# A depthwise convolution moved from two engines onto one, and eighteen PSUM copies moved to ScalarE

## The reference

```python
u, g, q, k, v, f = jnp.split(h, cuts, axis=-1)
a = u * jax.nn.sigmoid(g)
...
a_ext = jnp.concatenate([jnp.zeros((b, CONV_A_WIDTH - 1, CONV_A_CH), a.dtype), a], axis=1)
conv_out = conformer_tail(a_ext, w_dw_a[i], b_dw_a[i], ln_a_g[i], ln_a_b[i])
att = fox_prompt(q, k, v, lf)
```

## Time and profile before

| what | value |
|---|---|
| median of 3 runs | 2841.85 us (2841.03 to 2844.7) |
| the profiled execution, its own time | 2843.69 us |
| its span in the profile | 2842.0 us |
| busy: PE / DVE / ACT / POOL | 2632.0 / 1417.6 / 738.9 / 480.7 us |
| granted TensorE clock, mean | 0.953 |

### The profile page before, as it was taken

The page is one execution under the profiler, slowest core; times in us unless marked ns, Lnnn a source line. Parts: engine busy times, 40 slices in busy tenths (PEclk is TensorE's granted clock), DMA queues, the critical chain, the costliest instruction groups (busy, mean ns, idle before and its releaser), DMA issues.

```text
span 2842.0 us, 37619 instructions
## 1 busy us (share of the span) xinstructions
PE 2632.0 (93%) x15741; PEld 2537.0 (89%) x15741; DVE 1417.6 (50%) x1956; ACT 738.9 (26%) x1203; POOL 480.7 (17%) x436
## 2 busy tenths in 40 slices
PE   6987849897999999999999899989999999999995
PEld 5977737675999999999999789989999999999994
DVE  2699955555674333333333664457533333333356
ACT  3110135546342111111111431234311111111133
POOL 2189952221220000000000320023000000000022
PEclk8998968798999999999999999999999999999998
DMA  7111040016421111111111331133111111111131
GB/s 208 47 33 30 16 146 1 15 30 169 133 60 45 45 45 45 45 45 45 45 45 46 103 116 45 45 112 89 43 39 39 44 45 45 45 45 45 45 89 63
DMA packets 217916, 173.28 MB, mean 61 GB/s; under 512 B 9121, under 2 KB 195601, under 8 KB 217752
## 3 DMA queue, kind: packets, MB, share of 16 engines
q1 hardware_dynamic: 211488, 159.41, 19.1%
q0 software_dynamic: 4960, 11.49, 1.3%
q10 hardware_dynamic: 1320, 0.24, 0.1%
HBM read 152.45 MB, written 18.93 MB: 60 GB/s over the span
## 4 chain that ended last, share of the span: by engine, by line
PE 83%; DVE 9%; ACT 2%; issue 2%; DMA 1%; POOL 1%; SPq 1%; DVEq 0%; ACTq 0%; POOLq 0%
PE PS L664 24%; PE PS L665 24%; PE PS L666 24%; DVE CACC L1514 5%; PE PS L833 3%; PE PS L820 1%; PE PS L801 1%; DVE WLO L1430 1%; PE PS L805 1%; DMA RAW<-in_w_in_even 1%; DVE RSD L1709 1%; PE PS L678 1%; PE PS L679 1%; PE PS L672 0%; DVE Y L1717 0%
## 5 line engine op out<-in xcount | busy, mean ns | idle before, releaser
L664 PE MATMUL PS<-AH,WHI 128*128 128x368 f32 x3360 | 1126.3, 335 | 63.9 <-DVE QKV L1544 32.6
L665 PE MATMUL PS<-AL,WHI 128*128 128x368 f32 x3360 | 1119.9, 333 | 0.0
L666 PE MATMUL PS<-AH,WLO 128*128 128x368 f32 x3360 | 1115.5, 332 | 0.0
L664 PEld LDWEIGHTS PS<-AH,WHI 128*128 128x128 f32 x3360 | 639.8, 190 | 72.6 <-DVE QKV L1544 36.3
L665 PEld LDWEIGHTS PS<-AL,WHI 128*128 128x128 f32 x3360 | 638.5, 190 | 2.6 <-issue 0.6
L666 PEld LDWEIGHTS PS<-AH,WLO 128*128 128x128 f32 x3360 | 638.8, 190 | 0.0
L1774 DVE TENSOR_TENSOR HF<-S,PS 128x368 f32<-128x368 f32 x132 | 71.0, 538 | 678.5 <-ACT S L1067 678.5
L664 PE MATMUL PS<-HH,WHI 128*128 128x368 f32 x1056 | 353.4, 335 | 24.6 <-issue 16.7
L1052 ACT CAST WHI<-RAW 128x1024 fp32r<-128x1024 f32 x224 | 223.6, 1047 | 537.1 <-PE PS L666 530.7
L665 PE MATMUL PS<-HL,WHI 128*128 128x368 f32 x1056 | 352.8, 334 | 0.0
L666 PE MATMUL PS<-HH,WLO 128*128 128x368 f32 x1056 | 352.3, 334 | 0.0
(11 more groups left out here) (264 smaller groups left out, 2050.5 us busy)
## 6 DMA issues: line engine op xcount, KB each, us to landing
RAW<-in_w_ffn_gate SPq DMA_DIRECT2D x52, 512.0 KB, 3.9
RAW<-in_w_ffn_up SPq DMA_DIRECT2D x52, 512.0 KB, 4.9
RAW<-in_w_ffn_down SPq DMA_DIRECT2D x52, 512.0 KB, 3.6
RAW<-in_w_in_even SPq DMA_DIRECT2D x20, 512.0 KB, 5.0
Y<-x_spill SPq DMA_DIRECT2D x12, 736.0 KB, 8.2
RAW<-in_w_out_even SPq DMA_DIRECT2D x16, 512.0 KB, 4.6
RAW<-in_w_in_odd SPq DMA_DIRECT2D x16, 512.0 KB, 4.0
RAW<-in_w_out_odd SPq DMA_DIRECT2D x16, 512.0 KB, 4.8
```

The costliest lines, as they stand in the source:

```text
L664: pe.matmul(out, wh, xh, start=first, stop=False)
L665: pe.matmul(out, wh, xl, start=False, stop=False)
L666: return pe.matmul(out, wl, xh, start=False, stop=last)
```

## The change

VectorE convolves all four tiles, GpSimd none. The 18 copies of second tiles move from VectorE to ScalarE, which copies both banks of a unit one after the other. `TAPS` becomes 5; VectorE takes its 15 taps of a stage in one piece behind the stage's weight split, and one tap more behind the third unit of each of the gated stages 1 to 3. The wait for the small outputs that lie where the last tile of QKV goes (`sta_sent`) moves with the copies. GpSimd waits for four tiles, not three, before it clears its attention tiles.

```diff
-TAPS = 4
+TAPS = 5
...
-            k, acc, tmp, steps = HT - 1, HF[:].rearrange("p b n -> p (b n)"), S[:].rearrange("p b n -> p (b n)"), [0]
...
-                for j in range(CW):
-                    for out, part, src in pieces:
-                        if j == 0:
-                            pool_op(gp.tensor_scalar(out, src(j), row(k, R_DW), row(k, R_BDW), ALU.mult, ALU.add))
-                        else:
-                            pool_op(gp.tensor_scalar(part, src(j), row(k, R_DW + j), 1.0, ALU.mult, ALU.mult))
-                            pool_op(gp.tensor_tensor(out, out, part, ALU.add))
-                n = m + (NS * NQ if hi == TP else 0)
-                pool_op(gp.tensor_copy(AEXT[:, k, lo:lo + n], acc[:, 0:n]))
...
-            gp.wait_ge(conv_done, HT - 1)
+            gp.wait_ge(conv_done, HT)
...
+                    if it == 2 and j == 1:
+                        act.wait_ge(sta_sent, 16 * (1 + NS))
                     for c in range(NC):
                         gated(GU_QKV + 6 * it + 3 * j + c, (3 * j + c) % 2, ACT.Copy, S, QKV[:, 4 * it + 2 * j, chunk(c)])
+                        act.copy(QKV[:, 4 * it + 2 * j + 1, chunk(c)], PS[:, 2 * ((3 * j + c) % 2) + 1, 0:C]).then_inc(gu_free, 1)
...
-                for k in range(HT - 1):
+                for k in range(HT):
...
-                    for _ in range(3):
+                    for _ in range(3 + c // 2):
                         next(conv)
...
                 if q < 5:
                     split_stage(ST_QKV + q + 1)
-                else:
-                    dve.wait_ge(sta_sent, 16 * (1 + NS))
-                for c in range(NC):
-                    n = 3 * q + c
-                    dve.wait_ge(s_ready, GU_QKV + n + 1)
-                    dve.tensor_copy(QKV[:, 2 * q + 1, chunk(c)], PS[:, 2 * (n % 2) + 1, 0:C]).then_inc(gu_free, 1)
-                    for _ in range(TAPS):
-                        next(conv, None)
+                for _ in range(3 * TAPS):
+                    next(conv, None)
```

## The result

| | before | changed |
|---|---|---|
| median | 2843.27 us, 4 runs (2841.03 to 2845.89) | 2792.87 us, 4 runs (2792.73 to 2796.91) |
| span of the profiled execution | 2842.0 us | 2791.1 us |
| forecast | | 2800 us, 2794 to 2808 |

The ratio is 0.9826, with an interval of 0.9809 to 0.9843: faster by 50.4 us (1.7%), where 41.9 were forecast.

A forecast was written before the change was run, and what follows sets the result against it. VectorE, slowed by GpSimd's convolution, was taken to bound the query/key/value stage and tail. 40.9 us from its line plus 1.0 from the subtraction made 41.9 off the median of 2841.85: 2800 us, range 2794 to 2808.

The forecast's parts named there:

- The taps: VectorE's convolution in the query/key/value stages: a tap takes 1.53 us with GpSimd idle, against 2.57 beside GpSimd's convolution.
- VectorE's line: Sum of VectorE's work up to the tail: the tail begins at 309.7 us instead of 350.60, 40.9 us earlier.
- TensorE: Query/key/value units every 8.05 us, last done at 292.8; forget product lets the tail begin at 305.2, 4.5 before VectorE.
- ScalarE: Unit copies taken over in the query/key/value stages: 4.9 us of 24.15 a stage with casts, costing nothing.
- GpSimd and SP: Ahead of attention: earlier release counted as nothing, bounds 0 and 5.7 us, as the values load comes last.
- The subtraction: VectorE's 8-partition subtraction in the tail: 2.25 us beside GpSimd, 1.23 without it; 1.0 us gained, bounds 0 and 1.0.
- The slow taps without GpSimd: VectorE's taps stay at 2.57 us for reasons other than GpSimd: 98 us more than counted, 2899 us, slower; chance 0.03.
- the clock that stays at 0.92: TensorE's clock in the query/key/value stages doesn't rise, so 12.8 us stay: 2808 us; chance 0.06.
- the held start of attention: Attention's start is held by something that doesn't move, such as page-load traffic: 2842 us, no change; chance 0.03.
- the release as a bound: GpSimd's late release of attention was a bound beside the values load: up to 5.7 us more gain, 2794; chance 0.04.
- rival 4: GpSimd's late release of attention also bounded its start: up to 5.7 us more gain, 2794 us; chance 0.04.
- Attention and everything behind it move as one block.: From attention to the end, everything only starts earlier; all later stages keep their length, with no gain or loss.

The follow-up runs named there:

- The busy run: The changed kernel with GpSimd again running its 31 taps, on a constant tile with unused results: 2891.7 us, 1.0172 of before.
- clearings: The kernel before with 1, 2 or 4 more VectorE tile clearings at the tail's start: 2837.15, 2842.57, 2844.05 us; the changed one with 2 or 4: 2797.4, 2806.39.
- taps-alone kernel: The changed kernel with VectorE's unit copies put back between its taps, GpSimd still convolving nothing: 2811.21 us, 0.9879 of before.

## Why the prediction was right, and where not

- *The taps.* Right: 1.53 us start to start in the long chain too, 22.97 us for 15. The busy run shows the cause that the forecast had taken: GpSimd's activity alone costs a tap a further 1.0 us (2.62 against 1.58, the sums of the two means).
- *VectorE's line.* Right: 309.2 against 309.7. VectorE sets the end of the stage by its taps, as forecast.
- *TensorE.* Right in kind: no wait for VectorE is left from 147 to 310 us, units 8.05 us apart, clock 0.98. It began 2.4 us later than counted, as the clock was 0.77 in the 10 us ahead of the first unit, so that by the forecast's own count (295.17 + 12.4 = 307.6) its forget product was done 1.6 us ahead of VectorE, not 4.5. In other profiles the first unit came from 154.5 to 158.6 us (the kernel before, with and without clearings) and from 155.0 to 161.1 (the changed one and its variants); how much of the 2.4 us is chance stays open.
- *ScalarE.* Right: the copies cost nothing that shows; it idles 7.21 us between two units without weight casts.
- *GpSimd and SP.* Right: the earlier release gave nothing, since the values load came last (364.5, forecast 365.2). The run with the values load first shows that what hid it was that load alone.
- *The subtraction.* Right: 1.23 us, 1.0 gained.
- *The rivals.* The slow taps without GpSimd, the clock that stays at 0.92, the held start of attention and the release as a bound are each refuted by a row above. The time of 2792.87 lies near rival 4's 2794, but by luck: the release gave nothing.
- *The step that failed:* "Attention and everything behind it move as one block." The samples' part and the 2132 us behind it did, to 0.2 us. Attention did not: it took 220.1 us in place of 228.2, with equal instructions at a higher mean clock. By the profiled spans the gain is 50.9 us, 9.0 over the forecast's 41.9: 8.1 of them are attention, 0.7 lie ahead of it and 0.2 in the samples' part. The later runs put 219.5 to 228.2 us in place of the fixed block, for both kernels; what sets the length stays open. The forecast gave this term no error: with plus or minus 8 us for it the range would have held the time.

That the time came out below the range was in part chance. Five more runs of the changed kernel have a median of 2795.46 us, inside the range, and there the gain exceeds the forecast by 4.3 us, not 8.5; the two profiled attentions of the result lie near the two ends of what the runs showed.

A second slip: the forecast took the scatter of the kernel from three runs, 3.7 us wide. The 25 later runs of the unchanged kernel lie between 2836.11 and 2846.28 us, 10 wide, and the four of the taps-alone kernel are 13 wide. What one chooses as the median of a few runs can be off by several us.

## What to carry to other kernels

An engine that takes part of the work may slow the other by more than it takes: compare the same instruction's mean in a stretch where the second engine is idle with one where it works, before dividing work between them (here 1.58 us by the sum of a tap's two means against 2.57). Then look for what comes last behind the stage that shrinks; here a load that stood behind seventeen others in its queue hid 17 us, and moving it gave 11 to 14 us at the medians for no added instruction. And a part of the program that only moves in time may change in length where TensorE's clock changes in it (here attention, 219.5 to 228.2 us), so a block that "moves as one" deserves an error of its own.

## What the runs showed of the hardware

- A VectorE multiply-add of 128x1040 with two SBUF inputs took 1300 ns on average while GpSimd was idle, and 1919 to 2015 ns beside GpSimd's products and additions of 520 and 64 columns; on 128x64 it took 279 ns, and 608 to 649. GpSimd's product of 128x520 took 0.70 us alone and 1.57 beside the taps.
- One attention of 1383 matmuls took from 219.5 to 228.2 us in unchanged code, with mean granted clocks of 0.88 to 0.84. Two starts 1.8 us apart went with 228.2 and 222.3 us (408.2 and 410.0, the kernel before without and with two clearings), while the repeats of the kernel before and of the changed one gave their lengths again to 0.4 us. What sets it stays open.
- GpSimd's clearing of a tile, which reads nothing, went with a doubled VectorE copy from SBUF to SBUF, 1.47 against 0.73 us. It was seen once and not tried by itself.
